# A two-layer fp32 transformer block on one Trainium2 core: strips of 528 token columns cut to the 514 that are read, with the weights moved along

## The chip, the cores and the metric

The kernel runs on one core of a Trainium2 chip. The metric is the device time of one execution in microseconds (us); lower is better. In the text below PE is TensorE, DVE is VectorE, ACT is ScalarE, POOL is GpSimd, and SP is the engine that only issues DMAs here.

## The reference

Two blocks run one after the other on a sequence of 16 meta tokens followed by 512 real tokens, with 1024 features; only the 512 real tokens of the last result are returned. What matters for the change is which results read a meta token at all:

```python
def short_conv(u, w):            # width 3, causal: token t reads t, t-1, t-2
    ...
conv = cb * short_conv(cc * cx, conv_w)                     # first block
...
mix = (gate_sb * (sb @ w_sb_out[l]) + gate_gla * (o @ w_gla_out[l])) @ w_o[l]
h = h + _rmsnorm(mix, norm_mix_post[l])
hn = _rmsnorm(h, norm_ffn_pre[l])
up = hn @ w_ffn_up[l]
act = jax.nn.gelu(_causal_dwconv(up, conv_w[l], conv_b[l]), approximate=True)   # width 3 too
ffn = (act * (hn @ w_ffn_gate[l])) @ w_ffn_down[l]
h = h + _rmsnorm(ffn, norm_ffn_post[l])
return h[:, N_META:]
```

A causal convolution of width 3 over the real tokens (positions 16 to 527) reads positions 14 to 527. The attention branches (keys, values, recurrent states) read all 528 positions.

## The kernel before

Activations lie with features on the 128 partitions and tokens along the free dimension. A **strip** is one product of a 1024 x 128 piece of a weight matrix with all tokens: 8 chunks `c` of 128 input features. Every operand is split into a high and a low fp32r part, and three products are made per chunk: `wh` with `xh` (or `bh`), `wh` with `xl` (or `bl`), `wl` with `xh` (or `bh`). That gives 24 steps per strip. A strip whose meta tokens are not needed has `n = SEQ = 512` columns: one matmul of 512 columns per step (24 in all). A strip of all tokens has `n = T = 528` columns, which is more than a matmul may have, and so takes a **pair** of matmuls per step, of 256 and 272 columns (24 pairs, 48 matmuls), each with its own weight load of 128 columns. The function `pieces(b, n)` makes the two parts: its first piece is always 256 columns, and the second has the rest. It takes the last `n` of the 528 tokens, so with another `n` both pieces start at token `T - n`.

The strips are numbered through the whole program (`START`, `PHASES`), and strip `n` uses slot `n % 2` of three buffers of two slots each: `wraw` (filled by a DMA that SP issues), `wh` (written by ACT, `split_hi`, L568) and `wl` (written by DVE, `split_lo`, L1251). PE waits for `hi_done`, `lo_done` and for the eviction of the result before (`evicted`), then runs the strip (`strip`, L2189; special cases at L2210, L2263, L2601, L2652), and counts `mm_done`; DVE evicts the sums from PSUM (`scaled_by_root`, L1284, and others).

In the built program each partition holds `xh` at byte 4224, and each row of `xh`, `xl`, `bh`, `bl` is 2304 bytes long (nine times 256); `wh` is at byte 86208 and `wl` at 94400, with slots of 4096 bytes and chunks of 512 bytes. So a piece of a 528-column strip starts at 128 beyond a multiple of 256 bytes, a 512-column strip at 192 beyond one, and every chunk of weights at 192 beyond one. Below, the place of an operand within 256 bytes is called its **phase**. The quarter products of the first block (L2310, 256 columns each) have some operands in other buffers: `vt_r`, `qq_r`, `kk_r`, `mrg_r` and `xrows_r` have phase 128, whether they are moved or are weights.

Two buffers of the second block go out to DRAM and come back between their uses, on ACT's queue: `mrg` at L1040 and L1125.

The stretches that the change touches, by phase of the program: `conv_in` (first block's convolution inputs), the second block's gates in `sb_main`, its output products `sb_proj`, the last strips of `gla_main`, `gla_gates`, `gla_proj`, `w_o`, and the up strips of the three feed-forward groups `glu0up` to `glu2up`. The stretch behind `w_o` normalises, adds to the residual row by row (DVE, L2049 and L2051), and begins the feed-forward's first two strips as rows arrive (L2210).

Of the kernel before, what the change touches and what calls it, by code (L numbers as in the profile page):

```python
# [27 lines left out]
P = 128  # L28
# [6 lines left out]
SPLIT = SEQ // 2  # L35
EPS = 1e-6
# [40 lines left out]

def pos(base, k=0, i=0, step=2):

    return base + k + step * i, (base + k) // 2 + (step // 2) * i, (base + k) % 2  # L80
# [39 lines left out]
def build(nc, weights, cols, tables, consts, lam_rows, post_rows, x_t, meta2_t, wgk, gla_masks, res_dram,  # L120
          mrg_dram, tx_dram, out):
    ctx = ExitStack()
    with ctx:
# [6 lines left out]
        def shared(name, shape):  # L130

            with nc.sbuf_tensor(name, shape, F32) as plain:
# [9 lines left out]
        wh, wl = sb("wh", [P, 2, KC, P], F32R), sb("wl", [P, 2, KC, P], F32R)  # L142
# [33 lines left out]
        st_w = ([wh[:, k].rearrange("p k n -> p (k n)") for k in range(2)] + [flat(vtr)[:, 4 * D:5 * D]],  # L176
                [wl[:, k].rearrange("p k n -> p (k n)") for k in range(2)] + [flat(xrowsr)[:, 0:D]])
# [152 lines left out]

        RSTRIP, N_RET = START["ret_qkv"], 4 * RH + KC
# [34 lines left out]
        def wide_ap(n):  # L366

            return wide_at(4 + 2 * (n % 2), T)
# [30 lines left out]
        def gla_ap(j):  # L399

            n = GM + j
            return slot_ap(n % 2, T) if j < 6 or j >= 24 else lone_ap(n, T)
# [149 lines left out]
        def _(act):  # L552
# [10 lines left out]
            def split_hi(n, half, slot):  # L563
# [4 lines left out]
                nc.scalar.activation(wh[:, slot], wraw[:, slot], ACT.Copy).then_inc(hi_done, 1)  # L568
# [24 lines left out]
            for c in range(KC):  # L593
                act.wait_ge(x_in[c // 2], 16)
                hi_of(xh[:, c, :], res[:, c, :], wcol("norm1_w", c))
                if c == 0:
                    act.wait_ge(w_loaded[0], 16)
                    nc.scalar.activation(wh[:, 0, 0:2], wraw[:, 0, 0:2], ACT.Copy).then_inc(first_hi, 1)
                if c == 1:
                    nc.scalar.activation(wh[:, 0, 2:KC], wraw[:, 0, 2:KC], ACT.Copy).then_inc(hi_done, 1)  # L600
# [75 lines left out]
            def splits(B, count):  # L676

                with act.Fori(0, count // 2) as i:
                    for j in range(2):
                        split_hi(*pos(B, j + 1, i))  # L680

            def splits_and_root(B, src, n, dst, early=False):
# [25 lines left out]
                else:  # L708
                    root(two(dst), ps[:, 4:6, 0:HALF], 1.0 / D)
# [15 lines left out]
            def paired_gates(pairs, rows):  # L725

                nonlocal n_elsewhere
                for m, (q, n0) in enumerate(pairs):
# [4 lines left out]
                    for k in range(2):  # L733
# [3 lines left out]
                        nc.scalar.activation(wh[:, slot], wraw[:, slot], ACT.Copy).then_inc(hi_done, 1)  # L737
# [258 lines left out]
            for i in range(-3, 18):  # L996
# [34 lines left out]
                for c in {13: (0, 1), 14: (2, 3), 15: (4, 5), 16: (6,), 17: (7,)}.get(i, ()):  # L1031
                    n = SM + 12 + c
                    act.wait_ge(evicted[n % 2], n // 2 + 1)
                    nc.scalar.activation(mrg[:, c, :], mrg[:, c, :], ACT.Sigmoid).then_inc(sig_done, 1)
# [5 lines left out]
            act.dma_start(mrg_dram, mrg[:]).then_inc(mrg_saved, 16)  # L1040
# [30 lines left out]
            for i in range(-6, 27):  # L1071
# [51 lines left out]
                if i == 16:  # L1123
                    act.wait_ge(mrg_saved, 16)
                    act.dma_start(mrg[:], mrg_dram).then_inc(mrg_back, 16)  # L1125
# [3 lines left out]
                if 18 <= i < 22:  # L1129
                    for j in (2 * i - 36, 2 * i - 35):  # L1130
                        n = GM + 16 + j
                        act.wait_ge(evicted[n % 2], n // 2 + 1)
                        nc.scalar.activation(rg_rows[j], rg_rows[j], ACT.Silu).then_inc(silu_done, 1)
# [1936 lines left out]
```

## Time and profile before

| | |
|---|---|
| Median of 3 runs | 2100.34 us (2100.18 to 2100.38) |
| Time of the profiled execution | 2100.31 us |
| Its span, first to last instruction | 2098.5 us |
| PE busy | 2085.2 us (99%) |
| DVE busy | 1242.8 us (59%) |
| ACT busy | 831.2 us (40%) |
| Granted PE clock | 1.0 in every slice |

The profiled execution's own time is 1.8 us above its span; that is what lies around the span. Busy shares are averages over the program. Matmuls are pipelined, so the mean duration of one is longer than its share of the engine's time; the distance between the starts of successive groups gives the latter.

### The profile page before, as it was taken

To read this page: it belongs to the slowest core of one execution; us is meant where nothing else is said; L and a number is where in the kernel's file an instruction comes from. 1 tells how busy PE (TensorE), PEld (TensorE's weight loads), DVE (VectorE), ACT (ScalarE), POOL (GpSimd) and SP (SyncE) were. 2 spreads that over 40 slices of the span, in tenths; PEclk is the share of its full clock that TensorE was granted. 3 is DMA by queue.
4 is the path that set the end of the run, shared out by engine and by line. 5 is a ranking of instruction groups with operands and counts; after the bars stand their busy time and mean duration, and the time that the engine had idled before them with its cause. 6 is when DMAs were issued, how large, how long until landed. Compare 5 with 4: busy or idle time off the path is not lost.

```text
span 2098.5 us, 33880 instructions
## 1 busy us (share of the span) xinstructions
PE 2085.2 (99%) x13662; PEld 1850.1 (88%) x13662; DVE 1242.8 (59%) x1847; ACT 831.2 (40%) x1305; POOL 163.1 (8%) x146
## 2 busy tenths in 40 slices
PE   9999999999999999999999999999999999999998
PEld 8998988898888788899898888999999998889897
DVE  7775444565555555777664666367855557546364
ACT  4333222433444443434434566343424344222233
POOL 0012000030000000232120000022300000000000
PEclk9999999999999999999999999999999999999999
DMA  4343222522222233332323221231133322332322
GB/s 151 111 170 111 86 76 61 200 81 82 73 69 71 96 107 98 109 112 79 110 91 100 81 92 57 85 122 56 58 134 111 91 80 87 95 99 91 101 91 100
DMA packets 53563, 203.36 MB, mean 97 GB/s; under 512 B 6960, under 2 KB 7344, under 8 KB 52288
## 3 DMA queue, kind: packets, MB, share of 16 engines
q1 hardware_dynamic: 49248, 177.56, 26.4%
q10 hardware_dynamic: 3232, 20.80, 2.5%
q0 software_dynamic: 960, 3.24, 0.5%
q8 instruction: 91, 1.49, 0.3%
q14 instruction: 32, 0.26, 0.0%
HBM read 190.96 MB, written 10.62 MB: 96 GB/s over the span
## 4 chain that ended last, share of the span: by engine, by line
PE 93%; DVE 4%; ACT 2%; issue 0%; DMA 0%; DVEq 0%; SPq 0%; ACTq 0%
PE ps L2189 69%; PE ps L2310 7%; PE ps L2785 5%; PE ps L2652 1%; PE ps L2434 1%; PE ps L2459 1%; PE ps L2387 1%; PE ps L2717 1%; PE ps L2558 1%; DVE kk_r L1844 1%; PE ps L2473 1%; ACT kk L981 1%; ACT kk L982 1%; PE ps L2695 0%; PE ps L2539 0%; PE ps L2366 0%
## 5 line engine op out<-in xcount | busy, mean ns | idle before, releaser
L568 ACT ACTIVATE wh<-wraw 128x1024 fp32r<-128x1024 f32 x284 | 300.2, 1057 | 739.2 <-PE ps L2189 615.1
L1251 DVE TENSOR_TENSOR wl<-wraw,wh 128x1024 fp32r<-128x1024 f32 x298 | 366.2, 1230 | 129.4 <-ACT wh L568 125.8
L2189 PE MATMUL ps<-xh,wh 128*128 128x256 f32 (+2 forms) x1800 | 324.3, 325 | 0.7 <-DVE tmp L1284 0.5
L2189 PE MATMUL ps<-xl,wh 128*128 128x256 f32 (+2 forms) x1800 | 317.4, 321 | 0.0
L2189 PE MATMUL ps<-xh,wl 128*128 128x256 f32 (+2 forms) x1800 | 316.9, 321 | 0.0
L2189 PEld LDWEIGHTS ps<-xh,wh 128*128 128x128 f32 x1800 | 264.5, 188 | 29.4 <-issue 2.4
L2189 PEld LDWEIGHTS ps<-xl,wh 128*128 128x128 f32 x1800 | 265.7, 188 | 25.4
L2189 PEld LDWEIGHTS ps<-xh,wl 128*128 128x128 f32 x1800 | 265.7, 188 | 25.3
L2189 PE MATMUL ps<-bh,wh 128*128 128x512 f32 (+2 forms) x1296 | 231.6, 323 | 0.3 <-ACT wh L568 0.2
L2189 PE MATMUL ps<-bl,wh 128*128 128x512 f32 (+2 forms) x1296 | 228.0, 320 | 0.0
L2189 PE MATMUL ps<-bh,wl 128*128 128x512 f32 (+2 forms) x1296 | 228.0, 320 | 0.0
L2189 PEld LDWEIGHTS ps<-bh,wh 128*128 128x128 f32 x1296 | 190.2, 188 | 20.1 <-issue 1.6
L2189 PEld LDWEIGHTS ps<-bl,wh 128*128 128x128 f32 x1296 | 190.8, 188 | 17.8 <-issue 0.2
L2189 PEld LDWEIGHTS ps<-bh,wl 128*128 128x128 f32 x1296 | 190.8, 188 | 17.5
L1284 DVE TENSOR_TENSOR qq<-ps,rsq 128x528 f32<-128x528 f32 (+1 forms) x44 | 30.8, 700 | 95.4 <-PE ps L2189 95.2
L1284 DVE TENSOR_TENSOR tmp<-ps,rsq 128x528 f32<-128x528 f32 x31 | 21.9, 706 | 80.5 <-PE ps L2189 78.5
L576 ACT ACTIVATE bh<-hf 128x512 fp32r<-128x512 f32 (+1 forms) x30 | 18.9, 631 | 82.8 <-DVE hf L2098 46.6
L2785 PE MATMUL ps<-wh,bh 128*128 128x512 f32 x176 | 49.4, 389 | 0.0
L2785 PE MATMUL ps<-wh,bl 128*128 128x512 f32 x176 | 49.3, 389 | 0.0
L2785 PE MATMUL ps<-wl,bh 128*128 128x512 f32 x176 | 49.3, 389 | 0.0
L2932 POOL TENSOR_TENSOR qq<-qq,kk 128x512 f32<-128x512 f32 x3 | 5.0, 1659 | 564.9 <-DVE qq L2158 564.9
L1744 DVE SCALAR_TENSOR_TENSOR hf<-ps,rsq 128x512 f32<-128x512 f32 x32 | 22.0, 689 | 35.4 <-PE ps L2189 35.4
(533 smaller groups left out, 2773.1 us busy)
## 6 DMA issues: line engine op xcount, KB each, us to landing
wraw<-weights_dram SPq DMA_DIRECT2D x299, 512.0 KB, 3.6
qq<-weights_dram SPq DMA_DIRECT2D x12, 512.0 KB, 4.2
kk<-weights_dram SPq DMA_DIRECT2D x12, 512.0 KB, 4.5
hf<-tables_dram POOLq DMA_DIRECT2D x12, 264.0 KB, 3.0
res<-x_t_dram SPq DMA_DIRECT2D x4, 528.0 KB, 7.2
res<-x_t_dram ACTq DMA_DIRECT2D x1, 2112.0 KB, 9.2
res_dram<-res ACTq DMA_DIRECT2D x1, 2112.0 KB, 6.4
mrg_dram<-mrg ACTq DMA_DIRECT2D x1, 2112.0 KB, 9.0
```

The costliest lines, as they stand in the source:

```text
L568: nc.scalar.activation(wh[:, slot], wraw[:, slot], ACT.Copy).then_inc(hi_done, 1)
L981: link(nc.scalar.activation(sbt[e], sbt[e], ACT.Exp, scale=-1.0))
L982: nc.scalar.activation(sbt[e], sbt[e], ACT.Ln, bias=1.0).then_inc(slog_done, 1)
L1251: nc.vector.tensor_tensor(wl[:, slot], wraw[:, slot], wh[:, slot].bitcast(F32), ALU.subtract)\
L1284: return nc.vector.tensor_tensor(dst, src, row(rsq, n), ALU.mult)
L1744: nc.vector.scalar_tensor_tensor(out=hf[:, j, NM:T], in0=slot_ap(p0[2], SEQ), scalar=0.0, in1=rsq[:, NM:T], op0=ALU.max, op1=ALU.mult)\
L1844: ins = nc.vector.tensor_tensor(dst, src, hi.bitcast(F32), ALU.subtract)
L2189: last = nc.tensor.matmul(o, w[:, slot, c, :], a[:, c, tok], start=(k == 0), stop=(k == len(steps) - 1))
L2310: last = nc.tensor.matmul(st_bank(bank), w[:, c, :], a(c), start=(first and c == 0 and w is w_hi and a is acts[0]), stop=(c == 3 and w is ...
L2387: nc.tensor.matmul(ps[:, 5 + v, q0:SEQ], vt[:, t, f:f + P], at[:, t, q0:SEQ], start=(t == 0), stop=False)
L2434: ins = nc.tensor.matmul(ps[:, 2 + m, off:off + W], dq[h % 2][f, NM + P * b:NM + P * b + P], dk[h % 2][f, 0:W], start=True, stop=True)
L2785: last = nc.tensor.matmul(ps[:, 2 * t + h, :], a[:, c, NM + P * t:NM + P * t + P], w[:, slot, 4 * h:4 * h + 4, :].rearrange("p k n -> p (k ...
```

## The change

Strips whose meta tokens are read by a convolution alone, or by nothing, run on tokens 14 to 527: `USED = 514` columns in pieces of 256 and 258. Everything that DVE and ACT do with these rows is cut to the same 514 columns (`row(..., USED)`). The weights of such a strip are written 14 words (56 bytes) further into their slot, and a slot of `wh` and `wl` is 64 words (256 bytes) longer, so that slot 1 keeps its phase. `PLACE` says for each strip where its weights begin. A loop over strips must have one place for each of its steps, so the last pair of splits ahead of a phase with another place is written out behind the loop.

```diff
+USED = T - 14
+WIDTH = [SEQ] * NSTRIP
+for _name in ("ret_qkv", "diff_qkv", "sb_main", "gla_lr", "gla_main"):
+    WIDTH[START[_name]:START[_name] + dict(PHASES)[_name]] = [T] * dict(PHASES)[_name]
+for _name, _first in (("sb_main", 12), ("sb_proj", 0), ("gla_main", 16), ("gla_gates", 0), ("gla_proj", 0), ("w_o", 0)):
+    for _n in range(_first, dict(PHASES)[_name]):
+        WIDTH[START[_name] + _n] = USED
+for _n in range(24):
+    WIDTH[START["conv_in"] + _n] = SEQ if _n % 3 == 2 else USED
+for _g, _n in enumerate(FFN2_GROUPS):
+    WIDTH[START[f"glu{_g}up"]:START[f"glu{_g}down"]] = [USED, SEQ] * _n
+PLACE = [T - USED if w == USED else 0 for w in WIDTH]
+for _g in range(len(FFN2_GROUPS)):
+    PLACE[START[f"glu{_g}down"]] = T - USED
...
+def strip_at(w, n, slot):
+    o = PLACE[n if isinstance(n, int) else slot.first]
+    return w[:, int(slot), o:o + KC * P].rearrange("p (k n) -> p k n", k=KC)
...
-        wh, wl = sb("wh", [P, 2, KC, P], F32R), sb("wl", [P, 2, KC, P], F32R)
+        wh, wl = (sb(n, [P, 2, KC * P + 64], F32R) for n in ("wh", "wl"))
...
-                nc.scalar.activation(wh[:, slot], wraw[:, slot], ACT.Copy).then_inc(hi_done, 1)
+                nc.scalar.activation(strip_at(wh, n, slot), wraw[:, slot], ACT.Copy).then_inc(hi_done, 1)
...
-                with act.Fori(0, count // 2) as i:
+                with act.Fori(0, count // 2 - 1) as i:
                     for j in range(2):
                         split_hi(*pos(B, j + 1, i))
+                for k in (count - 1, count):
+                    split_hi(*pos(B, k))
...
-            act.dma_start(mrg_dram, mrg[:]).then_inc(mrg_saved, 16)
+            act.dma_start(row_all(mrg_dram), row_all(mrg)).then_inc(mrg_saved, 16)
...
-                    scaled_by_root(gate[:, :], slot_ap(p[0][2], T), T).then_inc(evicted[p[0][2]], 1)
+                    scaled_by_root(row(gate, USED), slot_ap(p[0][2], USED), USED).then_inc(evicted[p[0][2]], 1)
...
-                        last = nc.tensor.matmul(o, w[:, slot, c, :], a[:, c, tok], start=(k == 0),
+                        last = nc.tensor.matmul(o, strip_at(w, number, slot)[:, c, :], a[:, c, tok], start=(k == 0),
                                                 stop=(k == len(steps) - 1))
...
-                    strip(pos(B, k, i, 6), "x", SEQ if k % 3 == 2 else T)
+                    strip(pos(B, k, i, 6), "x", SEQ if k % 3 == 2 else USED)
...
-            strips(START["gla_proj"], KC, "x", T, ready=(op_ready, 7 * KC + SBP))
-            strips_and_sums(START["w_o"], "b", T, (in_ready, 4 * KC))
+            strips(START["gla_proj"], KC, "x", USED, ready=(op_ready, 7 * KC + SBP))
+            strips_and_sums(START["w_o"], "b", USED, (in_ready, 4 * KC))
```

With `WIDTH` as it stands, the strips of 514 columns are 16 of `conv_in`, 8 of `sb_main`, 4 of `sb_proj`, 8 of `gla_main`, 8 of `gla_gates`, 8 of `gla_proj`, 8 of `w_o` and 22 feed-forward strips: 82 strips. In the changed program their pieces start at phase 184 and their weights at phase 248; all other operands of the strips keep their phases. PE has as many instructions as before.

The first strip of the program on PE (chunk 0 and the beginning of chunk 1), before:

```order
L2263 MATMUL ps<-xh,wh 128x256
L2263 MATMUL ps<-xh,wh 128x272
L2263 MATMUL ps<-xl,wh 128x256
L2263 MATMUL ps<-xl,wh 128x272
L2263 MATMUL ps<-xh,wl 128x256
L2263 MATMUL ps<-xh,wl 128x272
```

and in the changed kernel:

```order
L2311 MATMUL ps<-xh,wh 128x256
L2311 MATMUL ps<-xh,wh 128x258
L2311 MATMUL ps<-xl,wh 128x256
L2311 MATMUL ps<-xl,wh 128x258
L2311 MATMUL ps<-xh,wl 128x256
L2311 MATMUL ps<-xh,wl 128x258
```

Nothing has moved on PE: the same matmuls stand in the same order, and the second of each pair has 14 columns less.

DVE at the evictions of `conv_in` (one chunk of the convolution: `gate` and `tmp` are the rows that it reads, `wl` the split of a strip's weights), before:

```order
L1284 TENSOR_TENSOR gate<-ps,rsq 128x528
L1350 TENSOR_TENSOR gate<-gate,rsq 128x528
L1251 TENSOR_TENSOR wl<-wraw,wh 128x1024
L1354 TENSOR_TENSOR tmp<-ps,gate 128x528
L1359 TENSOR_SCALAR hf<-tmp,col 128x512
L1361 SCALAR_TENSOR_TENSOR hf<-tmp,col,hf 128x512 x2
```

and in the changed kernel:

```order
L1321 TENSOR_TENSOR gate<-ps,rsq 128x514
L1321 TENSOR_TENSOR gate<-gate,rsq 128x514
L1288 TENSOR_TENSOR wl<-wraw,wh 128x1024
L1393 TENSOR_TENSOR tmp<-ps,gate 128x514
L1398 TENSOR_SCALAR hf<-tmp,col 128x512
L1400 SCALAR_TENSOR_TENSOR hf<-tmp,col,hf 128x512 x2
```

Three operations of a chunk are 14 columns shorter, and the split of the weights is as long as before.

ACT where `mrg` is saved, before:

```order
L568 ACTIVATE wh<-wraw 128x1024
L1034 ACTIVATE mrg<-mrg 128x528
L559 ACT_TABLE_LOAD
L568 ACTIVATE wh<-wraw 128x1024 x3
L1040 DMA mrg_dram<-mrg 128x4224
```

and in the changed kernel:

```order
L603 ACTIVATE wh<-wraw 128x1024
L1071 ACTIVATE mrg<-mrg 128x514
L594 ACT_TABLE_LOAD
L603 ACTIVATE wh<-wraw 128x1024 x3
L1077 DMA mrg_dram<-mrg 1024x1x514
```

The DMA moves 1024 runs of 514 words in place of 128 runs of 4224 words; its place in the queue is the same.

## Rows read from the trace of the kernel before

**Rows 1.** The page: busy times, and PE's granted clock in 40 slices.
```profile
PE 2085.2 (99%) x13662; PEld 1850.1 (88%) x13662; DVE 1242.8 (59%) x1847; ACT 831.2 (40%) x1305; POOL 163.1 (8%) x146
PEclk9999999999999999999999999999999999999999
```

**Rows 2.** Waits of PE, longest first: us in total, times, longest.
```profile
PE ps L2293 <- DVE kk L1287: 1.5, 1, 1.5
PE ps L2263 <- DVE wl L1296: 1.1, 1, 1.1
```

**Rows 3.** Windows: us, busy of PE, PEld, DVE, ACT, POOL, clock, DMA share, GB/s.
```profile
20.00:145.00 125.00, 125.00 (x870) 117.41 (x870) 89.07 (x117) 37.60 (x45) 12.92 (x8) 1.00 0.33 110
1310.00:1344.00 34.00, 34.00 (x287) 32.71 (x286) 10.35 (x12) 11.12 (x15) 0.00 (x0) 1.00 0.31 97
1570.00:1712.00 142.00, 142.00 (x1185) 142.00 (x1184) 71.06 (x88) 51.10 (x66) 0.00 (x0) 1.00 0.34 107
```

**Rows 4.** Timeline of PE in `conv_in`: start us, us, engine, line, operation.
```profile
28.61 2.08 PE L2189 MATMUL ps<-xl,wh 128*128 128x256 f32 x16
30.53 2.08 PE L2189 MATMUL ps<-xh,wl 128*128 128x256 f32 x16
...
38.21 1.99 PE L2189 MATMUL ps<-xh,wh 128*128 128x512 f32 x8
40.03 1.98 PE L2189 MATMUL ps<-xl,wh 128*128 128x512 f32 x8
```

**Rows 5.** Timeline of PE where one piece runs through before the other.
```profile
1201.77 1.10 PE L2601 MATMUL ps<-bh,wl 128*128 128x256 f32 x8
1202.71 1.15 PE L2601 MATMUL ps<-bh,wh 128*128 128x272 f32 x8
1203.70 1.15 PE L2601 MATMUL ps<-bl,wh 128*128 128x272 f32 x8
```

**Rows 6.** Timeline of PE in the quarter products, 256 columns each.
```profile
153.36 0.62 PE L2310 MATMUL ps<-xh,vt_r 128*128 128x256 f32 x4
153.81 0.62 PE L2310 MATMUL ps<-xl,vt_r 128*128 128x256 f32 x4
...
154.72 0.64 PE L2310 MATMUL ps<-qq_r,vt_r 128*128 128x256 f32 x4
155.20 0.64 PE L2310 MATMUL ps<-kk_r,vt_r 128*128 128x256 f32 x4
```

**Rows 7.** Groups of DVE from 1712 to 1736 us: busy, mean ns, idle before.
```profile
L2049 DVE SCALAR_TENSOR_TENSOR mrg<-mrg,col,gate 128x528 f32<-128x528 f32 x8 | 6.1, 761 | 0.5 <-ACT gate L584 0.5
L2051 DVE TENSOR_TENSOR res<-res,mrg 128x528 f32<-128x528 f32 x8 | 5.7, 708 | 0.3
L1271 DVE SCALAR_TENSOR_TENSOR xl<-res,col,xh 128x528 fp32r<-128x528 f32 x8 | 5.5, 762 | 0.0
```

**Rows 8.** Groups of DVE, and one of ACT, from 20 to 145 us.
```profile
L1251 DVE TENSOR_TENSOR wl<-wraw,wh 128x1024 fp32r<-128x1024 f32 x22 | 28.4, 1290 | 2.1 <-ACT wh L568 1.7
L1370 DVE TENSOR_TENSOR hf<-ps,hf 128x512 f32<-128x512 f32 x7 | 4.8, 690 | 3.9 <-PE ps L2189 3.9
L1284 DVE TENSOR_TENSOR gate<-ps,rsq 128x528 f32<-128x528 f32 x8 | 5.6, 704 | 6.0 <-PE ps L2189 4.4 <-ACT rsq L584 1.5
L568 ACT ACTIVATE wh<-wraw 128x1024 fp32r<-128x1024 f32 x21 | 22.1, 1054 | 32.7 <-PE ps L2189 31.1 <-DMA wraw<-weights_dram 1.6
```

**Rows 9.** DMAs that save `mrg` and bring it back, and DVE's operations next on `mrg`.
```profile
DMA to landing us min/median/max: 9.0/9.2/9.4
L1040 ACTq DMA_DIRECT2D mrg_dram<-mrg x1: 333/333/333, 1369.3 to 1369.3; - x1
L1125 ACTq DMA_DIRECT2D mrg<-mrg_dram x1: 327/327/327, 1562.0 to 1562.0; - x1
1420.60 1.25 DVE L1929 TENSOR_TENSOR_SCAN mrg<-res,kk 128x528 f32<-128x528 f32 x1
1626.91 0.71 DVE L1677 TENSOR_TENSOR mrg<-mrg,tmp 128x528 f32<-128x528 f32 x1
```

More of the change, by code:

```diff
@@ L708, in splits_and_root @@
                 else:
-                    root(two(dst), ps[:, 4:6, 0:HALF], 1.0 / D)
+                    root(two(row(dst, n)), ps[:, 4:6, 0:n // 2], 1.0 / D)
             def parts_of_rows(B, parts):
@@ L1033, in _ @@
                     act.wait_ge(evicted[n % 2], n // 2 + 1)
-                    nc.scalar.activation(mrg[:, c, :], mrg[:, c, :], ACT.Sigmoid).then_inc(sig_done, 1)
+                    nc.scalar.activation(row(mrg[:, c, :], USED), row(mrg[:, c, :], USED), ACT.Sigmoid).then_inc(sig_done, 1)
             table_set(LN_EXP)
@@ L1177, in _ @@
             act.wait_ge(sums_done, 4)
-            root(two(rsq[:, :]), ps[:, 4:6, 0:HALF], 1.0 / D)
+            root(two(row(rsq, USED)), ps[:, 4:6, 0:USED // 2], 1.0 / D)
             tile = 0
@@ L2043, in _ @@
             dve.wait_ge(in_ready, n_x)
-            summed_strips(START["w_o"], T, lambda c, src: nc.vector.tensor_copy(mrg[:, c, :], src))
+            summed_strips(START["w_o"], USED, lambda c, src: nc.vector.tensor_copy(row(mrg[:, c, :], USED), src))
             split_lo(*pos(START["w_o"], KC + 1))
@@ L2197, in glu_sums @@
                 for q in range(2):
-                    last = nc.tensor.matmul(ps[:, 4 + q, 0:HALF], ones, qq[:, 0, HALF * q:HALF * q + HALF], start=True,
+                    first = T - USED + USED // 2 * q
+                    last = nc.tensor.matmul(ps[:, 4 + q, 0:USED // 2], ones, qq[:, 0, first:first + USED // 2], start=True,
                                             stop=True)
@@ L2208, in product @@
                 def product(p, c, w, a):
-                    for tok, o in pieces(2 * p[2], T if p is up else SEQ):
-                        ins = nc.tensor.matmul(o, w[:, p[2], c, :], a[:, c, tok], start=(c == 0 and w is wh and a is xh),
+                    for tok, o in pieces(2 * p[2], USED if p is up else SEQ):
+                        ins = nc.tensor.matmul(o, strip_at(w, p[0], p[2])[:, c, :], a[:, c, tok],
+                                               start=(c == 0 and w is wh and a is xh),
                                                stop=(c == KC - 1 and a is xl))
@@ L2594, in strip_by_halves @@
                 pe.wait_ge(hi_done, n + 1)
-                for k, (tok, o) in enumerate(pieces(0, T)):
+                for k, (tok, o) in enumerate(pieces(0, WIDTH[n])):
                     pe.wait_ge(*waits[k])
```

129 lines of the change are left out of this document (73 added, 56 removed).

## The prediction

> **What bounds the kernel now.** I read the page first: PE is busy 2085.2 us, 99% of the span of 2098.5 us, at the full clock (2.4 GHz; 9 tenths or more granted in every slice, and 1.00 in every window) [rows 1, 3]. Then the waits: the two longest that PE has anywhere are 1.5 and 1.1 us, both at the start of the program [rows 2]. Then the windows of the stretches that the change touches: in 20 to 145 us (`conv_in`), 1310 to 1344 us (the gates of `sb_main`) and 1570 to 1712 us (`gla_gates`, `gla_proj`, `w_o`) PE is busy in all of the time, DVE in 71%, 30% and 50%, ACT in 30%, 33% and 36% [rows 3]. So PE's own instructions, one behind the other, set the end in all these places, and a matmul that takes less of PE's time shortens the kernel by that much, as long as DVE and ACT keep up.
>
> **What a pair of matmuls costs.** Busy durations of PE overlap, so I take distances between starts. In `conv_in` 16 matmuls, that is 8 pairs of 256 and 272 columns, start 1.92 us apart (28.61 to 30.53): 240.0 ns for a pair [rows 4]. Eight matmuls of 512 columns take 40.03 - 38.21 = 1.82 us: 227 ns each [rows 4]. At 2.4 GHz and one column in a clock, 528 columns are 220.0 ns and 512 are 213.3 ns: the rest is 20 ns for a pair and 14 ns for a lone matmul. Where the two pieces run apart, 8 of 256 columns take 1202.71 - 1201.77 = 0.94 us, 117.5 ns each, and 8 of 272 take 0.99 us, 123.8 ns each [rows 5]: 16 columns more cost 6.3 ns, against 6.67 ns by the clock. The time of a piece follows its columns, on top of about 11 ns that each matmul has.
>
> **The change part by part.**
>
> Columns of PE. The 82 strips have 24 pairs each: 1968 pairs. Each loses 14 columns of its second piece: 14 / 2.4 = 5.83 ns, if the 20 ns beside the columns stay. Sum: 1968 x 5.83 = 11.5 us. By the slope of rows 5 (0.39 ns a column) it would be 10.8 us; I take the clock, since the rows there are rounded to 0.01 us.
>
> The place of the operands. This is the unknown part. No fp32r stream of the trace starts anywhere but at a multiple of 64 bytes; now the pieces start at phase 184 and the weights at 248, both 56 bytes beyond one. What the trace does show is that the two places together matter. The quarter products at 153.36 us have moved columns and weights at different phases (192 and 128) and take 0.45 us for 4, 112.5 ns each; those from 154.72 us on have both at 128 and take 0.48 us for 4, 120 ns each [rows 6]. The pieces of rows 5, at 128 with weights at 192, lie between. The change moves both operands by the same 56 bytes, so their distance of 64 bytes stays, and I take the rest of 20 ns as unchanged. The bounds come from the same rows: if the new places turn out as the cheap ones, a pair costs 2 x 112.5 + 0.8 (two columns more than 512) = 225.8 ns, 14.2 less than now; if as the dear ones, 2 x 120 + 0.8 = 240.8 ns, 0.8 more than now. Over 1968 pairs that is 27.9 us less and 1.6 us more.
>
> The row stretch behind `w_o`. From 1715 to 1730 us PE is paced by DVE, which makes each of 8 rows in two operations of 761 and 708 ns, and then 8 low parts of 762 ns [rows 7]. An operation of 528 columns is 704 ns and one of 512 is 690 ns [rows 8], 0.9 ns a column; 24 operations shorter by 14 columns would give 24 x 12.3 = 0.3 us. I take 0.3 us; below, nothing; above, not more, since these are all the operations there.
>
> Sums. Six fp32 matmuls of 264 columns become 257 columns, some 0.1 us; I take it.
>
> Cost at nothing: DVE and ACT in the dense stretches. Their operations on these rows get shorter, so only the split of the weights could hurt, since it now writes 56 bytes off. In `conv_in` it is DVE 1290 ns and ACT 1054 ns a time [rows 8]. DVE's idle time in that window is 125.00 - 89.07 = 35.9 us over 22 splits [rows 3, 8]: each may take 1.6 us longer, more than twice its time, before PE has to wait for DVE. ACT, idle 87.4 us over 21 copies, has 4.2 us for each. The splits that left their loops are the same splits in the same order.
>
> Cost at nothing: the save and return of `mrg`. The return is issued at 1562.0 us and takes 9.4 us at most; DVE reads `mrg` first at 1626.91 us [rows 9]. With eight times as many runs it could take 6 times as long before anything waits. The save, issued at 1369.3 us, takes as long; DVE writes into `mrg` next at 1420.60 us [rows 9]. The wraw loads share the queues' engines, which are busy for 0.34 of that time [rows 3].
>
> Sum: 11.5 + 0.3 + 0.1 = 11.9 us off the profiled execution's own 2100.31 us (span 2098.5 and 1.8 around it), which is 0.03 us below the median of the three runs: **2088.4 us**. Its own range is 2087 to 2091 us; the upper end is the case in which the shorter piece is held by its weight load and gets no faster than a 256-column piece does in rows 5, 117.5 ns: a pair of 235 ns, 5.0 less, 9.8 us in all.
>
> **The rivals.**
>
> *Groups of four words.* The columns may come out of SBUF in aligned groups of four words. Before, both pieces began at the start of a group: 64 + 68 groups. Now each begins two words into one and touches 65: 130 groups, as 520 columns. A pair then loses 8 columns instead of 14: 3.33 ns, 6.6 us over all, and with the 0.4 us beside it 2093.3 us. Every row agrees with it and with the plain count of columns alike, since all fp32r streams of the trace begin and end on such places. This is the rule of the Trainium skill's page SBUF — State Buffer (in its section "A bandwidth-pool intuition that's wrong (but worth ruling out)"): 16-byte lines, full bandwidth within one, a penalty for each crossing to a new one. No row here shows a crossing in the middle of a stream to cost anything.
>
> *Groups of sixteen words; this is the one on the other side.* The same with 64 bytes. A piece of 256 or 258 columns that starts 56 bytes into a group touches 17 groups; the pair needs 34 where it needed 16 + 17 = 33. If a group costs 16 clocks, a pair costs 6.67 ns more: 13.1 us slower, with 0.4 us back: 2113.0 us. For it: 240.0 ns is 576 clocks and 227 ns about 544, both multiples of 16 [rows 4], and the phases that matter in rows 6 differ by 64 bytes. Against it: the pieces apart, 117.5 and 123.8 ns, are 282 and 297 clocks and no such multiples [rows 5], and 112.5 ns is 270 [rows 6]; and all column counts are multiples of 16, which explains round sums without any groups. It decides from about 14 columns' worth of loss in a pair on.
>
> *The dear phase.* The pieces and weights may meet at their new places as the equal phases of rows 6 do: 240.8 ns a pair, 1.6 - 0.4 = 1.2 us slower, 2101.5 us. For it: the spread within rows 6 has more than one cause. Against it: the distance of 64 bytes stays.
>
> *The cheap phase.* The other end: between 2086 us and 2100.3 - 27.9 - 0.4 = 2072 us. Only rows 6 speak for it.
>
> **How the numbers follow.** Forecast 0.51; groups of four 0.14; the dear phase 0.12; groups of sixteen 0.17; the cheap phase 0.06. 0.2% of this kernel is 4.2 us, about what a measurement can tell from no change here, so forecast, groups of four and cheap phase are faster (0.71), the dear phase is the same (0.12), groups of sixteen slower (0.17). The range runs from 2079 us, which holds half of the cheap phase, to 2103 us, above the dear phase; it leaves out 0.17 and 0.03.
>
> **What the profile of the changed kernel would show.** The distance of eight pairs in `conv_in` gives it at once: 1.873 us if only columns count (234.2 ns a pair), 1.893 us with groups of four, 1.973 us with groups of sixteen, 1.927 us for the dear phase. The 512-column strips must stay at 1.82 us for 8, or the longer slots have an effect of their own. PE's longest waits should stay those at the start, and the window that was 1570 to 1712 us shorter by its 24 whole strips x 24 x 5.83 ns = 3.4 us. DVE's `wl` should stay near 1290 ns in `conv_in`. The prediction is wrong if the pair's price moves by other than its columns, or if DVE or ACT get slower at 56 bytes off by so much that PE waits for `hi_done` or `lo_done`.

## The result, and the profile after

The changed kernel takes 2105.61 us (median of 11 runs, 2105.40 to 2105.84); the kernel before, run beside it, 2100.34 us (11 runs). The ratio is 1.0025, with a 95% interval of 1.0017 to 1.0033: it is 5.3 us slower, where 11.9 us faster was forecast, and it lies outside the range. The profiled execution has a span of 2103.9 us, 5.4 us more than before.

The page and the windows of the changed kernel (busy us of PE, PEld, DVE, ACT and POOL in each window, then the clock, the DMA share and GB/s), the counterparts of [rows 1, 3]:

```profile
PE 2091.3 (99%) x13662; PEld 1855.2 (88%) x13662; DVE 1242.1 (59%) x1847; ACT 830.4 (39%) x1305; POOL 165.2 (8%) x146
20.00:145.00 125.00, 125.00 (x866) 117.49 (x866) 88.45 (x116) 37.64 (x45) 12.80 (x8) 1.00 0.34 110
1310.00:1344.00 34.00, 34.00 (x283) 32.71 (x283) 10.28 (x12) 11.02 (x15) 0.00 (x0) 1.00 0.29 94
1570.00:1712.00 142.00, 142.00 (x1167) 141.76 (x1166) 69.85 (x88) 52.24 (x70) 0.00 (x0) 1.00 0.34 113
```

PE is still never idle there and at the full clock, with the same 13,662 matmuls. But in the same 125 us it now gets 866 of them started instead of 870, and in 142 us 1167 instead of 1185: each one takes longer on average. The longest waits of PE, against [rows 2], and the two weight splits from 20 to 145 us, against [rows 8]:

```profile
PE ps L2341 <- DVE kk L1324: 1.5, 1, 1.5
PE ps L2619 <- ACT gate_r L1025: 0.9, 4, 0.3
...
L1288 DVE TENSOR_TENSOR wl<-wraw,wh 128x1024 fp32r<-128x1024 f32 x22 | 28.7, 1307 | 1.8 <-ACT wh L603 1.3
L603 ACT ACTIVATE wh<-wraw 128x1024 fp32r<-128x1024 f32 x21 | 22.1, 1054 | 33.5 <-PE ps L2234 32.0 <-DMA wraw<-weights_dram 1.5
```

Nothing new is waited for, and writing the weights 56 bytes further costs DVE and ACT next to nothing. The whole loss is in the price of a pair. The timeline of PE in `conv_in`, against [rows 4], and in `gla_gates`:

```profile
26.81 2.08 PE L2234 MATMUL ps<-xh,wh 128*128 128x256 f32 x16
28.73 2.11 PE L2234 MATMUL ps<-xl,wh 128*128 128x256 f32 x16
...
36.52 2.11 PE L2234 MATMUL ps<-xh,wl 128*128 128x256 f32 x16
...
40.29 1.98 PE L2234 MATMUL ps<-xl,wh 128*128 128x512 f32 x8
42.10 1.99 PE L2234 MATMUL ps<-xh,wl 128*128 128x512 f32 x8
```
```profile
1584.22 2.11 PE L2234 MATMUL ps<-bl,wh 128*128 128x256 f32 x16
...
1601.74 2.11 PE L2234 MATMUL ps<-bl,wh 128*128 128x256 f32 x16
```

From 28.73 to 36.52 us there are four rows of 8 pairs: 7.79 us / 32 = **243.4 ns a pair**, 3.4 ns more than before, although it has 14 columns fewer. In `gla_gates` nine rows, 72 pairs, take 17.52 us: 243.3 ns. The 512-column products stay at 1.81 us for 8. Not every pair pays this: the first row of a strip that follows a 512-column strip still takes 1.92 us (26.81 to 28.73), 240.0 ns a pair. There are about 28 such strips, so some 220 pairs of the 1968. The other 1750 or so x 3.4 ns are 5.9 us more; less the 0.4 us that the narrower rows of DVE and the sums were counted to give back (the three groups of [rows 7] now have means of 748, 695 and 749 ns, 13 ns less each), that makes 5.5 us, against 5.4 measured.

Where the two pieces run apart, as in [rows 5], the strips that the change touches show the same from another side:

```profile
1292.96 1.12 PE L2649 MATMUL ps<-bh,wl 128*128 128x256 f32 x8
1293.92 1.12 PE L2649 MATMUL ps<-bh,wh 128*128 128x258 f32 x8
1294.88 1.12 PE L2649 MATMUL ps<-bl,wh 128*128 128x258 f32 x8
```

Eight products take 0.96 us, 120.0 ns each, with 256 columns and with 258. The 256-column piece, whose width did not change, cost 117.5 ns before (its rows now give 118.8 to 120.0 ns).

In what follows a price is always such a distance of starts, over 8 to 72 pairs. The starts are rounded to 0.01 us, so a price over 8 pairs is uncertain by about 1.3 ns and one over 32 pairs by 0.3 ns. "Place" is where an operand starts within 256 bytes: before, both moved pieces started at 128 and the weights at 192; the change puts the pieces at 184 and the weights at 248. For the 512-column products both the columns and the weights are at 192, before and after. Prices of a pair without a stretch named are from `conv_in`.

### The profile page after: what moved, and what is told of

Read it like the earlier page. It is cut to its first block, busy times and chain, and to the rows that moved or that the text cites. A ratio compares the mean times of both kernels' runs of the same rounds, so it can differ in the third digit from the quotient of the medians.

```text
span 2103.9 us, 33866 instructions
## 1 busy us (share of the span) xinstructions
PE 2091.3 (99%) x13662; PEld 1855.2 (88%) x13662; DVE 1242.1 (59%) x1847; ACT 830.4 (39%) x1305; POOL 165.2 (8%) x146
## 4 chain that ended last, share of the span: by engine, by line
PE 93%; DVE 4%; ACT 2%; issue 0%; DMA 0%; SPq 0%; DVEq 0%; ACTq 0%
PE ps L2234 69%; PE ps L2358 7%; PE ps L2834 5%; PE ps L2700 1%; PE ps L2482 1%; PE ps L2507 1%; PE ps L2435 1%; PE ps L2765 1%; PE ps L2606 1%; DVE kk_r L1884 1%; PE ps L2521 1%; ACT kk L1018 1%; ACT kk L1019 1%; PE ps L2743 0%; PE ps L2587 0%; PE ps L2414 0%
## 5 line engine op out<-in xcount | busy, mean ns | idle before, releaser
L2234 PE MATMUL ps<-xh,wh 128*128 128x256 f32 (+3 forms) x1800 | 324.5, 325 | 0.5 <-DVE tmp L1321 0.4
L2234 PE MATMUL ps<-xl,wh 128*128 128x256 f32 (+3 forms) x1800 | 318.5, 322 | 0.0
L2234 PE MATMUL ps<-xh,wl 128*128 128x256 f32 (+3 forms) x1800 | 318.3, 322 | 0.0
L2234 PE MATMUL ps<-bh,wh 128*128 128x512 f32 (+3 forms) x1296 | 232.2, 323 | 0.3 <-ACT wh L603 0.2
L2234 PE MATMUL ps<-bl,wh 128*128 128x512 f32 (+3 forms) x1296 | 228.7, 320 | 0.0
L2234 PE MATMUL ps<-bh,wl 128*128 128x512 f32 (+3 forms) x1296 | 228.7, 320 | 0.0
L1321 DVE TENSOR_TENSOR qq<-ps,rsq 128x512 f32<-128x512 f32 (+2 forms) x44 | 30.7, 698 | 96.2 <-PE ps L2234 96.1
L1321 DVE TENSOR_TENSOR tmp<-ps,rsq 128x514 f32<-128x514 f32 (+1 forms) x31 | 21.6, 697 | 81.7 <-PE ps L2234 79.7
```

The source lines that it names most:

```text
L1321: return nc.vector.tensor_tensor(dst, src, row(rsq, n), ALU.mult)
L2234: last = nc.tensor.matmul(o, strip_at(w, number, slot)[:, c, :], a[:, c, tok], start=(k == 0), stop=(k == len(steps) - 1))
```

## The experiments

**The weights back at their old place.** All else as the change.

```
-PLACE = [T - USED if w == USED else 0 for w in WIDTH]
+PLACE = [0 for w in WIDTH]
```

> The changed kernel with the weights of the 514-column strips left at their old place (phase 192), slots as long as in the change; the moved columns still start 56 bytes beyond a multiple of 64. In the changed kernel eight pairs of 256 and 258 columns start 1.947 us apart in conv_in, 243.4 ns a pair, against 240.0 before. Theory M, the unaligned start of the moved columns costs it: 243 ns a pair as now, about 2105.6 us. Theory W, the unaligned weights cost it: 234 ns a pair, about 2088 us. Theory R, what counts is how far moved columns and weights lie apart, and the change kept that well: now 8 bytes apart instead of 64, so the dear price of equal phases, 246 to 254 ns a pair, 2111 to 2127 us. Theory S, a piece of some 256 columns is held at about 121 ns by something else: 243 ns, 2105.6 us.

Measured: 2101.22 us, ratio 1.0004 (0.9995 to 1.0014). The price is (36.20 - 28.49) / 32 = 240.9 ns:

```profile
28.49 2.09 PE L2232 MATMUL ps<-xl,wh 128*128 128x256 f32 x16
...
36.20 2.09 PE L2232 MATMUL ps<-xh,wl 128*128 128x256 f32 x16
```

No theory had this price. Moving the weights along cost 2.5 ns a pair, 4.4 us over all, so keeping the distance to the moved columns did not help. Without it the pair still costs 240.9 ns, against 240.0 before, although it has 14 columns fewer; its moved columns still start at 184 here. The 512-column products stay at 226.6 ns in these longer slots.

**The moved columns back at 128, on tokens 0 to 513.** Weights at their old place too; in `conv_in` and in the up strips of the last part the pieces start at token 0, at place 128 as before the change (the last 14 tokens are not computed there). `first` is 0 in these strips. So this is the kernel before in both places, with 258 columns in the second piece instead of 272.

```
+            if n == USED:
+                return [(slice(first, first + SPLIT), ps[:, b, SPLIT:2 * SPLIT]),
+                        (slice(first + SPLIT, first + n), ps[:, b + 1, 0:n - SPLIT])]
...
```

> The changed kernel with all weights at phase 192, and in conv_in and the up strips of the feed-forward groups (but for the two that start the first group) the 256 and 258 columns are taken from token 0 on instead of 14, so they start at phase 128 as before the change; those strips then use tokens 0 to 513, which are not the ones that the reference needs, the number of columns and all else is the changed kernel's. Theories M and R: the pair costs its columns, 234 ns in those strips. Theory W: 234 ns too, there and in all other strips of 514. Theory S: 240 ns or more there, though aligned. Groups of sixteen words (a 258-column piece touches 17 groups, as one of 272 does): 240 ns, no less than before.

Measured: one run, 2097.55 us.

```profile
28.23 2.04 PE L2236 MATMUL ps<-xl,wh 128*128 128x256 f32 x16
...
35.76 2.05 PE L2236 MATMUL ps<-xh,wl 128*128 128x256 f32 x16
```

The price is (35.76 - 28.23) / 32 = 235.3 ns there, and stays near 241 ns in the other strips of 514. Against the run before, with the weights at 192 in both, the start of the columns (184 or 128) is worth 5.6 ns a pair. Against the kernel before (240.0 ns), with both places the same, 14 columns fewer are worth 4.7 ns. That rules out theory W (the others do not fall), theory S (at least 240 ns) and the groups of sixteen words (a piece of 258 columns from place 128 touches 17 groups, as one of 272 does: 240 ns).

**The kernel before, with its weights alone 56 bytes further.**

```
-        sb("ahead_of_weights", [P, 16])
+        sb("ahead_of_weights", [P, 30])
...
-        sb("behind_weights", [P, 48])
+        sb("behind_weights", [P, 34])
```

> The kernel before, only its spacer ahead of the weights 14 words longer and the one behind 14 shorter: all weights lie 56 bytes on (phase 248), every moved column stays. Theory M: 240 ns a pair of 256 and 272 and 227 ns for 512 columns, as before, 2100.3 us. Theory W: each weight load touches one group of 64 bytes more, 3 to 7 ns a matmul: 246 to 254 ns a pair, 230 to 234 for 512. Theory R: prices move, by up to 7 ns a matmul either way, the 512-column strips' with them. Theory S: as before.

Measured: one run, 2139.65 us, 39 us slower than before with not one column changed:

```profile
28.86 2.12 PE L2189 MATMUL ps<-xl,wh 128*128 128x256 f32 x16
...
36.69 2.12 PE L2189 MATMUL ps<-xh,wl 128*128 128x256 f32 x16
...
40.51 2.03 PE L2189 MATMUL ps<-xl,wh 128*128 128x512 f32 x8
42.38 2.03 PE L2189 MATMUL ps<-xh,wl 128*128 128x512 f32 x8
```

A 512-column product rises from 227 to 1.87 us / 8 = 233.8 ns and a pair from 240.0 to 7.83 us / 32 = 244.7 ns. So the place of the stationary operand alone changes the price, and theories M and S, by which nothing would move, fell.

**The cut of the pieces at token 272, weights at several places.** The pieces are 258 columns from 184 and 256 from 192.

```
+            if n == USED:
+                return [(slice(T - n, T - SPLIT), ps[:, b, SPLIT - 2:2 * SPLIT]),
+                        (slice(T - SPLIT, T), ps[:, b + 1, 0:SPLIT])]
...
```

> The changed kernel with the pieces cut at token 272 instead of 270: 258 columns from token 14 (unaligned start, ending on a multiple of 64 bytes) and then 256 columns from token 272 (phase 192), same 514 columns. Weights of these strips at phase 192 in conv_in, 248 in sb_main, sb_proj and gla_main, 64 in gla_gates, gla_proj and w_o, 128 in the feed-forward. Theory M with groups of sixteen words: 17 + 16 groups instead of 17 + 17, so one group, 6.7 ns, less than the changed kernel has at the same weight place: about 237 ns. Theory W: 234 in conv_in, gates and feed-forward, 243 in sb_main. Theory R: prices that go with the weights' place, lowest where neither piece has the weights' phase. Theory S: 243 everywhere.

Measured: one run, 2096.29 us, less than both kernels. 237.5 ns a pair with the weights at 192 (`conv_in`), 238.3 ns at 64 (`gla_gates`), about 237 ns at 128 (feed-forward), and 235.4 ns at 248 in `sb_main`: the place that is dear in the change is cheap beside another cut. That looked like a rule for a best place, so the next run used it everywhere.

**The square: cut at 270 or 272, weights at 248 or 192.** The change with the cut of the run before as its only edit, and the same with `PLACE` all 0.

> The change in every part, its weights 56 bytes further on included, with one edit: the pieces are tokens 14 to 271 and 272 to 527 (258 and 256 columns) instead of 14 to 269 and 270 to 527. The second piece then starts where a 512-column product starts, at place 192 of 256 bytes. Theory A (the moved columns are paid by the groups of 64 bytes that they touch, 16 clocks or 6.7 ns each, and the two starts also act on each other): the pair costs 235.4 ns wherever it stands, as it did in three stretches of the run with mixed places, against 243.4 ns in the change; 1968 pairs x 8.0 ns = 15.7 us less than the change: span 2088.2, time about 2090, faster than the kernel before by 0.4 to 0.5%. Theory B (weights that start inside a group of 64 bytes cost a group more, as in the kernel before with its weights shifted): the pair costs 560 + 16 clocks = 240.0 ns, time about 2099. Theory C (the few stretches were cheap for another reason, their bank or their order): between, 2092 to 2096.

> As the run above (258 and 256 columns, cut at token 272), but with all weights at their old place, 192 of 256 bytes. With the change, the change with its weights put back, and the run above it makes a square: cut at 270 or 272, weights shifted or not. If cut and weights act each by itself: moving the weights back was worth 2.4 ns a pair at the cut at 270, so the pair would be 235.4 - 2.4 = 233.0 ns here, time about 2086. Theory A, in which it is the places of the two to each other that count: 238 to 239 ns a pair, as in the first stretch of the run with mixed places, time 2094 to 2097. Theory B: 560 clocks, 233.3 ns a pair, time 2086 to 2087.

Measured: 2097.83 us (0.9988, 0.9979 to 0.9997) with the weights at 248, and 2096.72 us (0.9983, 0.9974 to 0.9993) with them at 192. The first missed its 2090 by 8 us, and its timeline shows where; the two pairs of rows are the same code in the same stretch with the same places:

```profile
1528.23 2.04 PE L2237 MATMUL ps<-bl,wh 128*128 128x258 f32 x16
1530.11 2.05 PE L2237 MATMUL ps<-bh,wl 128*128 128x258 f32 x16
...
1538.35 2.08 PE L2237 MATMUL ps<-bl,wh 128*128 128x258 f32 x16
1540.27 2.08 PE L2237 MATMUL ps<-bh,wl 128*128 128x258 f32 x16
```

8 pairs take 1.88 us (235 ns) in one strip and 1.92 us (240.0 ns) in a later one, and 240.0 ns it is then through `gla_gates`, `gla_proj` and `w_o`; in `conv_in` it is 238.4 ns. So a pair of places does not have one price. It is not the slot either: the strips between 1508 and 1532 us, which use both slots in turn, all run at 235 ns, and those from 1538 us on at 240 ns. What decides is not shown. The 11 executions of this kernel took 2096.86 to 2098.54 us, where those of the change lie within 0.44 us, so the price may also differ from one execution to the next. With the weights at 192 the price is 237.8 ns in both stretches. The square in ns a pair in `conv_in`: cut 270, 243.4 (weights at 248) and 240.9 (192); cut 272, 238.4 and 237.8. Weights at 248 instead of 192 cost 2.5 ns at one cut and 0.6 ns at the other, so the two don't simply add, and the expectation that they would (233.0 ns, 2086 us) fell. So did theory B's 233.3 ns; theory A's 2094 to 2097 us for the second run was met.

**Other places of the weights, for the change's cut and for the kernel before.** `PLACE` is set by stretch, for all strips of a stretch, those of 512 columns included. The second kernel is the changed one with `USED = T`, so it has the longer slots; its pairs are of 256 and 272 columns, not of 264 as its expectation says.

> The change with its cut at token 270 (both pieces start at place 184), and the weights at other places in each stretch: at 184 in the first stretch and in the first group of the last part (the same as the moved columns), at 128 in the second mixed stretch and the second group of the last part, at 64 in the third, at 56 in the fourth, at 224 in the last group. Theory B (only whether the weights start on a group of 64 bytes counts): 240.9 ns a pair at 128 and 64, 243.4 ns at 184, 56 and 224. Theory A (the places to each other count): the price differs among the aligned ones or among the shifted ones, by up to 16 clocks a pair (234 to 247 ns); equal places (184 and 184) dearest, since the quarter products at equal places took 120.0 ns against 112.5 to 117.9 at others. The time by either: 2098 to 2108. 512-column products of the first stretch, weights at 184 and columns at 192: 233.3 ns by B.

> The kernel before as to its columns (528 columns in two pieces of 264 everywhere, 512 in one), with the weights at other places, all on a group of 64 bytes: at place 0 in the first stretch, at 64 in the first half of the first wide part and at 128 in its second half, at 128, 64 and 0 in the second layer's stretches, and at 128, 64 and 0 in the three groups of the last part. Theory B: nothing changes, 240.0 ns a pair and 226.6 ns a 512-column product everywhere, time 2100. Theory A: some place is cheaper or dearer by a group; if the weights' old place 192, which is also that of the 512-column products, were a dear one as equal places are in the quarter products, the 512-column products would fall to 220.0 ns (528 clocks) at 0, 64 or 128, and the time by some 10 us. The slots that are 256 bytes longer are in it too; by themselves they should cost nothing.

Measured: 2109.17 us (1.0042, 1.0027 to 1.0057), 1.2 us above what either theory allowed, and 2122.48 us (1.0106, 1.0087 to 1.0124), where theory B had 2100. With the cut at 270 a pair costs 238.8 ns with the weights at 184, where both pieces start, against 240.0 at 56 and at 128, 240.9 at 192, about 241 at 224, 242 at 64 and 243.4 at 248. With 512 columns at place 192 a product costs 226.6 ns with the weights at 192, 228.9 at 128, 232.4 at 64, and 233.3 at 0, 184, 224 and 248. A pair of the kernel before rises from 240.0 to 246.6 ns with the weights at 0, a place as even as any, and to 9.76 us / 40 = 244.0 ns with the weights at 128, which is just where its own pieces start (`sb_main`, the last two rows):

```profile
29.30 2.13 PE L2236 MATMUL ps<-xl,wh 128*128 128x256 f32 x16
...
37.19 2.13 PE L2236 MATMUL ps<-xh,wl 128*128 128x256 f32 x16
...
41.03 2.03 PE L2236 MATMUL ps<-xl,wh 128*128 128x512 f32 x8
42.90 1.79 PE L2236 MATMUL ps<-xh,wl 128*128 128x512 f32 x7
```
```profile
1330.28 2.12 PE L2236 MATMUL ps<-bh,wh 128*128 128x256 f32 x16
...
1340.04 2.12 PE L2236 MATMUL ps<-bh,wl 128*128 128x256 f32 x16
```

So a start on 64 or 256 bytes is not what makes weights cheap (theory B fell). The same place as the moved columns is the cheapest of those tried for the 512-column products (192 with 192) and for the pieces of the change (184 with 184), where theory A had it dearest. But it is dear for the pieces of the kernel before (128 with 128), as it is in [rows 6]. No one rule of places fits all of them.

**A narrower second piece.** Weights at 192, cut at 270; the columns behind the numbers in the expectation are left out.

```
...
-                    for tok, o in rows:
+                    for tok, o in (narrow if k else rows):
```

> The change with its weights at their old place and its cut at token 270, but the second piece of each pair (all but the first product of a strip) has fewer columns, so that the last tokens of these strips are not summed up: 250 in the first stretch, 244 in the second layer's first mixed stretch, 242 in the next, 226 in the strips after it, and 244, 242 and 228 in the three groups of the last part. The piece starts 56 bytes into a group of 64, so 244 to 258 columns touch 17 groups, 228 to 242 touch 16, and 226 touch 15. With 258 columns the pair cost 240.9 ns. Theory of groups (what is paid is the groups touched, 16 clocks each): about 241 ns at 250 and at 244, 234 at 242 and at 228, 227 at 226: steps, and no slope between them. Theory of columns (2.4 columns a ns): 237.6 at 250, 235.1 at 244, 234.2 at 242, 228.4 at 228, 227.6 at 226.

Measured: one run, 2092.95 us. A pair costs 241.9 ns with 250 columns in the second piece, no less than with 258, then 233.4 ns with 244, with 242, with 228 and with 226. That is neither theory: 250 and 244 touch equally many groups and differ by 8 ns, and from 244 down 18 columns are worth nothing at all. So the price does not follow the columns in general, though it fell by 4.7 ns from 272 to 258 columns at the old places.

**Both pieces narrow.** The same edit on both pieces.

> The change with its cut at token 270, but in all products of a narrowed strip except its first both pieces take fewer columns (the rest of the tokens is not summed up in these strips): 128 and 128 in the first stretch, 200 and 200 in the second layer's first mixed stretch, 128 and 128 in the next, 240 and 240 in the strips after it, 200, 128 and 240 in the three groups of the last part. Weights at place 192 in the first stretch and in the first group of the last part, at 248 in all others. A strip changes its columns from product to product, its weights are loaded anew for each piece. Theory of the load (a piece of up to about 244 columns costs what bringing in its 128 x 128 weights costs, 116.7 ns, and no less): 233.3 ns a pair at 240, 200 and 128 columns alike, at either place of the weights, or one group (6.7 ns a load) more at 248, 240 to 246.7. Theory of columns: 200 ns and more at 240 columns, 167 at 200, 107 to 130 at 128, so the time falls by 60 us and more. The 2.4 columns a ns of my sum would be right only under the second.

Measured: one run, 2076.68 us. The timelines with 128 + 128 columns (weights at 192), 200 + 200 (at 248) and 240 + 240 (at 248); a row that says 256 begins with the strip's one full product:

```profile
28.41 1.95 PE L2248 MATMUL ps<-xl,wh 128*128 128x128 f32 x16
30.20 1.95 PE L2248 MATMUL ps<-xh,wl 128*128 128x128 f32 x16
31.98 1.97 PE L2248 MATMUL ps<-xh,wh 128*128 128x256 f32 x16
```
```profile
1322.64 1.95 PE L2248 MATMUL ps<-bl,wh 128*128 128x200 f32 x16
1324.43 1.95 PE L2248 MATMUL ps<-bh,wl 128*128 128x200 f32 x16
1326.21 1.96 PE L2248 MATMUL ps<-bh,wh 128*128 128x256 f32 x16
```
```profile
1587.94 1.97 PE L2248 MATMUL ps<-bl,wh 128*128 128x240 f32 x16
1589.75 1.98 PE L2248 MATMUL ps<-bh,wl 128*128 128x240 f32 x16
1591.56 1.99 PE L2248 MATMUL ps<-bh,wh 128*128 128x256 f32 x16
```

3.57 us for 16 pairs: 223.1 ns a pair, 111.6 ns a product, with 128 and with 200 columns, and 226.3 ns with 240. So a product with fresh 128 x 128 weights takes 111.6 ns with 200 columns as with 128. Half the columns save 18 ns of the 240.9 that the full pieces cost at the same places. With 128 and with 200 columns the price is the same with the weights at 192 and at 248 (223.1 to 223.4 ns a pair in the five stretches with such strips): the place costs only where more columns are moved. The theory of columns falls for good. Of the theory of the load the flat price holds, at 111.6 in place of 116.7 ns; that a place costs a group more does not. Other products of the same traces show such a price too. Here are products of 128 columns in the changed kernel, two of them in each row:

```profile
1537.36 0.39 PE L2745 MATMUL ps<-qq,gate 128*128 128x128 f32 x2
1537.58 0.39 PE L2743 MATMUL ps<-tmp,vt 128*128 128x128 f32 x2
1537.81 0.39 PE L2745 MATMUL ps<-qq,gate 128*128 128x128 f32 x2
```

0.45 us for four of them, 112.5 ns each, where 128 columns alone, at one in a clock of 2.4 GHz, are 53 ns. That it is the loading that takes this time, and not another cost that each product has, I infer; no run here changed the size of the weights. The Trainium skill, page TensorE: Matmul & The Clock Gate, section "LDWEIGHTS (loading the stationary operand)", gives a load as its columns over 1.2 in ns, by which I estimate 106.7 ns for 128; the measured floor is 5 ns above it. The same page's section "Back-to-back issue gap" has 81 ns a product at 128 columns and 131 ns at 512 in a stream of loads and products; here it is 111.6 and 226.6 ns, and the measurement decides.

**Equal places, and the best one found.** The change with 62 words (weights at 184, as both pieces) in place of 14; then the cut at 272 with the weights at other places by stretch; then that cut with 48 words throughout (weights at 128). The edit of the first:

```
-PLACE = [T - USED if w == USED else 0 for w in WIDTH]
+PLACE = [62 if w == USED else 0 for w in WIDTH]
...
```

> The change with one number other: the weights of the narrowed strips go 248 bytes further into their slots instead of 56, so that they start at place 184 of 256, just where both moved pieces start. The cut stays at token 270. Theory of equal places (weights and moved columns at the same place of 256 bytes are the cheapest pair of places, as 192 with 192 is in the 512-column products, which cost 226.6 ns there and 228.5 to 233.4 ns at six other places): 238.7 ns a pair everywhere, as in the first stretch of the run with other places; 1968 x 4.7 ns = 9.3 us less than the change, time 2096 to 2097. Theory that only whether the weights start on a group of 64 bytes counts: 243.4 ns a pair as in the change, time 2105 to 2106.

> The cut at token 272 (258 columns from place 184, then 256 from place 192) with the weights of the narrowed strips at other places: at 184 in the first stretch, in the third mixed stretch and in the first group of the last part, at 128 in the second mixed stretch, at 0 in the strips before the last part, at 224 in its second group and at 128 in its third. With the weights at 192 a pair cost 238.2 ns, at 248 first 235.5 and later 238.3 to 240.0 ns. Theory of equal places: 184 and 192 are equally good (each is equal to one of the two pieces), 238 ns, and 0, 128 and 224 are dearer, 239 to 242 ns. Theory that a pair of places has a price only together with what ran just before it (it falls into one of several steady beats and stays there until an interruption): the prices lie between 235 and 240 ns without order by place, and more than one price appears at one place. Time by either 2095 to 2100.

> The likeliest best version so far: the cut at token 272 and the weights of all narrowed strips 192 bytes further (place 128), all else as the change. Where these places stood in earlier runs a pair cost 236.5 to 237.9 ns, against 243.4 in the change, 240.0 in the kernel before and 238.2 with the weights at 192. If that price holds everywhere: 1968 x 3.2 ns = 6.3 us less than the kernel before plus the 0.4 to 1.2 us that its narrower rows give, less 2 us for the first products of the 512-column strips beside them (230.0 instead of 226.6 ns); time 2094 to 2096, faster than before by 0.2 to 0.3%. If a pair of places has more than one steady beat, as 184 and 192 with 248 had (235.5 and 240.0), some stretch stands at 240.0 and the time is 2096 to 2098.

Measured: 2098.66 us (0.9993, 0.9983 to 1.0002) for equal places, 238.8 ns a pair in both stretches. The price came as expected; the time is 1.7 us above its range, in part because the pairs that follow 512-column strips never cost 243.4 ns in the change. With the cut at 272 and other places 2095.00 us (0.9976, 0.9966 to 0.9986), with pairs at 238.0 (weights at 184), 236.7 (128), 236.6 (224) and 240.0 ns (0); some strips at the borders of its stretches read weights from another place than where they were written, which changes values and not the work. The prices are from the profiled execution of 2097.51 us; six of the eight executions took 2094.80 to 2095.07 us, the other two 2097.15 and 2097.51. Here the theory of equal places fell: 128 and 224, which equal neither piece, are cheaper than 184, which equals one. And with the weights at 128 throughout **2095.09 us** (0.9974, 0.9965 to 0.9984), which beats both kernels:

```profile
1583.16 2.05 PE L2237 MATMUL ps<-bh,wh 128*128 128x258 f32 x16
...
1600.20 2.05 PE L2237 MATMUL ps<-bh,wh 128*128 128x258 f32 x16
```

17.04 us for 72 pairs: 236.7 ns. The other stretches lie between 236.6 and 237.5 ns, and the expected time of 2094 to 2096 us was met. It is 10.5 us off the change for two numbers, the cut and the place.

## Why the prediction was wrong

**What bounds the kernel** was right: PE is busy without a gap before and after, nothing new is waited for, and the time follows the pairs' price.

**"Their distance of 64 bytes stays, and I take the rest of 20 ns as unchanged"** is the step that failed, and it turned the sign. The rest was 20 ns before, and is 243.4 - 514 / 2.4 = 29.2 ns after. The runs take the change apart in `conv_in`, one edit at a time: 14 columns fewer at the old places give -4.7 ns (240.0 to 235.3), the start of the moved columns from 128 to 184 costs +5.6 (to 240.9), and the weights from 192 to 248 cost +2.5 (to 243.4). The sum is +3.4 ns, the measured loss. In each of the four traces the price is the same in the feed-forward as in `conv_in` (8 pairs take 1.92 us before, 1.88 or 1.89 on tokens 0 to 513, 1.92 or 1.93 with the weights back, 1.94 or 1.95 in the change), so no second price, as one pair of places had in the square, is mixed into the steps. The two places together cost 8.1 ns a pair, where the prediction had nothing. Its bounds for this step, 225.8 and 240.8 ns, both came from [rows 6], two prices of other products, and the measured one lies above both. Equal distance is not what counts: at 64 bytes apart a pair of 514 columns costs 235.3 ns in one case and 243.4 in the other.

**"The time of a piece follows its columns, on top of about 11 ns that each matmul has"** gave nearly the right number here and is wrong as a rule. Of 5.83 ns a pair, 4.7 came at the old places. By that price the 1968 pairs would have given 9.2 us, and with the 0.4 us beside it the time would have been 2090.7 us, inside the prediction's own range; this is an estimate from the run on tokens 0 to 513, and no run has those places and the right tokens. But the rule came from one slope, between 256 and 272 columns [rows 5], and does not hold below: 250 columns in the second piece cost no less than 258, 226 no less than 244, and a product with new weights has a floor of 111.6 ns. The prediction named the case of a piece "held by its weight load" at 117.5 ns, a pair of 235 ns. That number was met at the old places, by luck: the floor lies 5.9 ns lower, so the floor is not what holds a piece at 117.5.

**Groups of sixteen words**, the rival on the other side, had the right sign and twice the size: 246.7 ns, 6.7 more than before, against 3.4 measured. It is not the mechanism: 250 and 244 columns touch equally many groups and differ by 8 ns, and 272 and 258 columns from place 128 do too and differ by 4.7 ns. **Groups of four words** would have left 236.7 ns; the rule that the prediction cites for it stands in the "Specifications (TRN2)" section of that page of the Trainium skill. **The cheap phase** had 225.8 ns; no pair with its full 514 columns came below 235 in any run. **The dear phase** has 240.8 ns, close to the 240.9 with the weights back. That is chance: the places are 184 and 192 there, not equal. Where they were made equal at 184, the pair cost 238.8 ns.

**Cost at nothing** for DVE, ACT and the DMAs of `mrg` was right: 1307 and 1054 ns for the splits, and no wait.

What stays open is what links the places to the price. The runs show that the places of weights and moved columns act together: no difference between weights at 192 and at 248 with 200 columns and fewer, and several ns with 256 and more. They show that equal places are cheapest at 192 (512 columns) and at 184 (256 and 258, cut at 270) but dear at 128 (256 and 272), and that one pair of places can stand at 235 or at 240 ns in one execution. Why is not shown.

## What to carry to other kernels

When a narrower range of columns also moves the start of an operand, count the two apart: here the columns were worth 4.7 ns a pair and the new starts cost 8.1. Where PE runs without a gap, the places within 256 bytes at which weights and moved columns start are a setting that was worth up to 1.9% here, and a shift of both by the same number is not neutral. No simple rule of alignment or of equal places came out of these runs, so measure a few over whole strips, together with the cut of the pieces. And look in the trace for the narrowest products of the same kind before counting what fewer columns are worth: their distance is the floor, and no cut in columns gets below it.

## What the runs showed of the hardware that was not expected

- 128 and 200 columns with fresh 128 x 128 weights both cost 111.6 ns a product; 240 columns cost 113.1.
- 56 bytes further for all weights of the kernel before, and nothing else, cost 39 us of 2100 (1.9%; one run).
- Weights at place 0, aligned to 256 bytes, are no better than at 184 or 248 for 512 columns at 192: 233.3 ns against 226.6 at equal places.
- Equal places are no safe choice: with both at 128 a pair of 256 and 272 columns cost 244.0 ns, against 240.0 with the weights at 192.
- The same code at the same places ran at 235 and at 240 ns a pair within 10 us of one execution.
- A second piece of 250 columns was no cheaper than one of 258 (241.9 and 240.9 ns), while one of 244 was 7.5 ns cheaper than that of 258.
